# First block: modulation rows summed over partitions by accumulating DMAs on GpSimd, through a scratch row, in place of TensorE

## The reference

```python
cond = jax.nn.silu(c)                       # (1, 1024)
for l in range(2):
    mod = cond @ ada_w[l] + ada_b[l]        # 1024 x 9216
    sh1, sc1, g1, sh2, sc2, g2, sh3, sc3, g3 = jnp.split(mod, 9, axis=-1)
    hn = rms_norm(h, norm_g[l, 0]) * (1 + sc1) + sh1
    h = h + 0.5 * g1 * swiglu(hn, ffn1_w_in[l], ffn1_w_out[l])
    hn = rms_norm(h, norm_g[l, 1]) * (1 + sc2) + sh2
    h = h + g2 * (mixers(hn @ w_in[l]) @ w_out[l])
    hn = rms_norm(h, norm_g[l, 2]) * (1 + sc3) + sh3
    h = h + 0.5 * g3 * swiglu(hn, ffn2_w_in[l], ffn2_w_out[l])
```

## Time and profile before

| | us |
|---|---|
| median of 3 runs | 2239.07 |
| lowest and highest run | 2237.37, 2240.9 |
| profiled execution, device time | 2241.53 |
| its span, first to last instruction | 2239.8 |
| TensorE busy | 2187.2 |
| VectorE busy | 1589.0 |
| ScalarE busy | 1097.1 |
| GpSimd busy | 52.5 |

### The profile page before, as it was taken

One profiled execution on the slowest core, in us unless ns is written; L12 is line 12 of the kernel. 1 busy time (PEld: TensorE's weight loads), 2 busy tenths in 40 slices (PEclk: granted clock), 3 DMA queues, 4 the chain that ended last, 5 costly groups with the idle time before them and its releaser, 6 DMA issues.

```text
span 2239.8 us, 31962 instructions
## 1 busy us (share of the span) xinstructions
PE 2187.2 (98%) x11867; PEld 1843.9 (82%) x11867; DVE 1589.0 (71%) x1904; ACT 1097.1 (49%) x1288; POOL 52.5 (2%) x94
## 2 busy tenths in 40 slices
PE   7999999999999999999999999999999999999998
PEld 6887887887787897888788799978878879998887
DVE  5887898876777699665655778675575567867555
ACT  4344665444444466444544566554454446465443
POOL 1000010000000010000000000000000000000000
PEclk9999999999999999999999999999999999999999
DMA  8986576995687566665555464455556556435553
GB/s 283 345 315 219 162 225 209 327 315 173 242 291 244 155 212 197 229 224 192 185 190 192 154 167 132 151 188 187 187 173 203 187 169 169 133 132 170 191 191 104
DMA packets 325042, 454.56 MB, mean 203 GB/s; under 512 B 32722, under 2 KB 270040, under 8 KB 324952
## 3 DMA queue, kind: packets, MB, share of 16 engines
q1 hardware_dynamic: 320952, 440.98, 59.9%
q0 software_dynamic: 3728, 11.31, 1.7%
q10 hardware_dynamic: 272, 1.05, 0.1%
HBM read 449.91 MB, written 1.05 MB: 201 GB/s over the span
## 4 chain that ended last, share of the span: by engine, by line
PE 88%; DVE 6%; ACT 2%; issue 2%; DMA 1%; SPq 1%; DVEq 0%; ACTq 0%
PE ps L627 20%; PE ps L629 20%; PE ps L628 20%; PE ps L620 5%; PE ps L621 5%; PE ps L622 5%; PE ps L799 2%; DVE wlo L1993 1%; PE ps L781 1%; PE ps L784 1%; PE ps L782 1%; PE ps L718 1%; PE ps L1074 1%; ACT whi L1368 1%; DMA arena<-in_ada_w_dram 1%
## 5 line engine op out<-in xcount | busy, mean ns | idle before, releaser
L1993 DVE TENSOR_TENSOR wlo<-raw,whi 128x2048 fp32r<-128x2048 f32 x348 | 791.6, 2278 | 346.9 <-ACT whi L1368 345.4
L1368 ACT ACTIVATE whi<-raw 128x2048 fp32r<-128x2048 f32 x346 | 660.2, 1910 | 282.6 <-PE ps L629 241.5
L627 PE MATMUL ps<-whi,xl 128*128 128x512 f32 x1472 | 590.5, 401 | 0.0
L629 PE MATMUL ps<-whi,xh 128*128 128x512 f32 x1472 | 574.2, 390 | 0.0
L628 PE MATMUL ps<-wlo,xh 128*128 128x512 f32 x1472 | 574.0, 390 | 0.0
L627 PEld LDWEIGHTS ps<-whi,xl 128*128 128x128 f32 x1472 | 276.6, 188 | 61.6 <-issue 4.6
L629 PEld LDWEIGHTS ps<-whi,xh 128*128 128x128 f32 x1472 | 276.4, 188 | 60.0
L628 PEld LDWEIGHTS ps<-wlo,xh 128*128 128x128 f32 x1472 | 276.7, 188 | 57.5 <-issue 3.3
L627 PE MATMUL ps<-whi,hidl 128*128 128x512 f32 x640 | 252.1, 394 | 1.0 <-DVE hidl L2188 1.0
L620 PE MATMUL ps<-xl,whi 128*128 128x256 f32 x864 | 249.3, 288 | 1.6 <-DVE wlo L1993 1.6
L629 PE MATMUL ps<-whi,hidh 128*128 128x512 f32 x640 | 249.2, 389 | 0.0
(11 more groups left out here) (405 smaller groups left out, 2331.6 us busy)
## 6 DMA issues: line engine op xcount, KB each, us to landing
raw<-in_ffn_w_in_dram SPq DMA_DIRECT2D x176, 512.0 KB
arena<-in_ada_w_dram SPq DMA_DIRECT2D x144, 512.0 KB, 6.0
raw<-in_w_in_dram SPq DMA_DIRECT2D x54, 1024.0 KB
raw<-in_ffn_w_out_dram SPq DMA_DIRECT2D x44, 1024.0 KB
raw<-in_w_ffn_gate_dram SPq DMA_DIRECT2D x88, 512.0 KB
raw<-in_w_ffn_up_dram SPq DMA_DIRECT2D x88, 512.0 KB
raw<-in_w_ffn_down_dram SPq DMA_DIRECT2D x44, 1024.0 KB
raw<-in_w_out_dram SPq DMA_DIRECT2D x16, 1024.0 KB
```

Source lines behind the costliest of these rows:

```text
L627: pe.matmul(o, al, wh, start=start, stop=False, **kw)
L629: return pe.matmul(o, ah, wh, start=False, stop=stop, **kw)
L1368: act.activation(whi[:, k % 3, :], raw[:, k % 3, :], ACT.Copy).then_inc(hi_done, 1)
L1993: tt(a[0], a[1], a[2].bitcast(F32), ALU.subtract).then_inc(lo_done, 1)
```

## The change

In the feed-forwards n = 0, 2, 3 and 5 the sum over partitions is made by `fold_sums` on GpSimd. A DMA with an addition adds rows 64 to 127 of the accumulators onto rows 0 to 63, the next adds rows 32 to 63 onto 0 to 31, and so on, seven times, each step waiting for the one before. Row 0 is then stored to a scratch row in device memory, and each of its 1024-number pieces is loaded into all 128 partitions of its destination: shift, gate, and for the scale the buffer `adag`. `acc` is handled as two pieces of 1536 columns and `accg` as one of 1024, so that a step has three DMAs in n = 0 and 2, two in n = 3 and one in n = 5. VectorE waits for the rows after `lower_last(1)` and makes `gain` there, in one operation of 128 x 1024. The factor of 0.5 moves into `residual`. The matmuls, the waits for their banks, and the copies out of PSUM go in the feed-forwards; the mixers keep theirs.

```diff
-        SUMS = (0, 4, 10, 14, 20, 26, 30)
+        SUMS = (0, 4, 4, 8, 8, 8, 12)
+        LAID = {0: 64, 2: 128, 3: 176, 5: 192}
+        FOLDED = (0, 16 * 24, 16 * 48, 16 * 64)
...
-                if m not in (2, 5):
-                    pe.wait_ge(mod_read, SUMS[m] + q)
                 pe.matmul(ps[:, sumb(m, q), :], ones_row[:, :], acc[:, 512 * q:512 * q + 512], start=True,
...
-                    modulation(m, q)
...
-                    if q < 2:
-                        gate0(n, q)
...
-                    group(0, k, GROUPS - 3, (lambda q: modulation(m, q)) if m else None)
-                group(0, k + 3, GROUPS - 2, between1 if n == 0 else (lambda q: gate0(n, q) if q < 2 else None) if n in GATED else None, True)
+                    group(0, k, GROUPS - 3)
+                group(0, k + 3, GROUPS - 2, between1 if n == 0 else None, True)
...
-                if m:
-                    pe.wait_ge(mod_read, SUMS[m] + 6)
-                if n and n in GATED:
-                    pe.wait_ge(gate0_read, 2 * GATED.index(n) + 2)
...
-                st(tt(rtmp[:, f, :], o, gate[:, n % 2, 512 * f:512 * f + 512], ALU.mult))
+                st(stt(rtmp[:, f, :], o, 1.0 if n % 3 == 1 else 0.5, gate[:, n % 2, 512 * f:512 * f + 512], ALU.mult,
+                       ALU.mult))
...
                 lower_last(1)
-                if n in GATED:
-                    dve.wait_ge(gate0_read, 2 * GATED.index(n) + 2)
+                if n in LAID:
+                    dve.wait_ge(laid, LAID[n])
+                if m:
+                    dve.wait_ge(gain_loaded, 16 * m)
+                    st(stt(gain[:, :], adag, 1.0, gain[:, :], ALU.add, ALU.mult))
...
+            row_sums = nc.dram_tensor("row_sums", (4, 4 * D), F32, kind="Internal").ap()
+
+            def fold_sums(n):
+
+                e, m = list(LAID).index(n), n + 1 if n < 5 else 0
+                k, pieces = FOLDED[e], []
+                if m:
+                    until(adam_used, ADAM[m + 1] + 2)
+                    pieces += [(0, acc[:, 0:1536]), (1536, acc[:, 1536:3072])]
+                if n in GATED:
+                    until(adag_used, KC * (GATED.index(n) + 1) + 1)
+                    pieces += [(3 * D, accg)]
+                for half in (64, 32, 16, 8, 4, 2, 1):
+                    for _, t in pieces:
+                        pool.dma_start(t[0:half], t[half:2 * half], accum_op=ALU.add).then_inc(folded, 16)
+                        k += 16
+                    until(folded, k)
+                for at, t in pieces:
+                    pool.dma_start(row_sums[e:e + 1, at:at + t.shape[1]], t[0:1, :]).then_inc(folded, 16)
+                    k += 16
+                until(folded, k)
+                rows = [(3, gate[:, n % 2, :])] if n in GATED else []
+                if m:
+                    rows += [(0, shift), (1, adag), (2, gate[:, m % 2, :])]
+                for q, o in rows:
+                    pool.dma_start(o, row_sums[e, D * q:D * q + D].partition_broadcast(P)).then_inc(laid, 16)
+                until(laid, LAID[n])
...
                 if n == 5:
                     late_consts()
+                if n in LAID:
+                    fold_sums(n)
```

More of the change, by code:

```diff
@@ L220, in program @@
         mod_summed, mod_read = sem("mod_summed"), sem("mod_read")
-        gate0_summed, gate0_read = sem("gate0_summed"), sem("gate0_read")
+        folded, laid = sem("folded"), sem("laid")
         gain_loaded, gate_loaded = sem("gain_loaded"), sem("gate_loaded")
@@ L904, in between1 @@
                     if q == 3:
-                        pe.wait_ge(gate0_read, 2)
                         turn_setup(2)
@@ L1499, in summed @@
                 act.wait_ge(mod_summed, SUMS[m] + q + 1)
[L1500 to L1509, removed]
+                act.activation(shift[:, 512 * q:512 * q + 512], ps[:, sumb(m, q), :], ACT.Copy).then_inc(mod_read, 1)
             def ffn(L, n, j, k0):
@@ L1552, in ffn @@
                     setup_kept_out(0)
-                if m:
-                    summed(m, 0)
-                    summed(m, 1)
                 upper(g)
@@ L1562, in ffn @@
                     setup_exps()
[L1563 to L1567, removed]
+                    setup_kept_out(1)
                 hi(L, k + 7)
-                if n in GATED:
-                    gate0(n, 0)
-                    gate0(n, 1)
                 upper(g + 1)
@@ L2236, in ffn @@
                 product(g + 1, 0)
-                if m:
-                    summed(m, 2)
                 product(g + 1, 1)
-                if m:
-                    summed(m, 3)
                 lo(L, k + 6)
```

## The result

The changed kernel is slower by 3.5%, and its time lies outside the range given.

What follows compares the result with a forecast made beforehand. TensorE, busy 98% of the span, was taken to bound the kernel, with VectorE leading at boundaries. Folds against windows, savings and gain gave +5.5 us, the clock 3.5, total +9.0 on 2239.1: 2248 us, range 2221 to 2285.

Steps and rivals of the forecast that it cites:

- What goes: TensorE's sums in sub-blocks 0, 2, 3 and 5: 24 pairs of matmuls go at 0.86 us, 20.6 us.
- What comes on VectorE: Gain's multiply-add in sub-blocks 0, 2, 3: 1.28 us each, 3.84 us on the path; residual's two multiplications cost nothing.
- The window: From last addition to VectorE's last split: 42.0, 40.6, 42.25 and 36.2 us in sub-blocks 0, 2, 3 and 5.
- the formula: A sub-block's change is the larger of minus its saving and fold minus window, plus 1.28 us where gain is made.
- The length of a fold: On GpSimd, nine dependent steps: 44.8 us with three pieces, 38.6 with two, 28.9 with one.
- The prediction's own sign of being wrong: In GpSimd's chain, a small step under 3.2 us or over 5 would show the prediction wrong.
- A rule against the rows: Skill's 2.0 us plus bytes at 436 GB/s per DMA: folds of 36.2 and 29.5 us, sum -13.2 us, 2226 us.
- Additions that read twice: In the large halvings an addition also reads its destination; the middle was taken, 17.6 us together for three pieces.
- The clock: Behind late folds of sub-blocks 0 and 2 TensorE runs at a lower clock: 3.5 us, ends 0 and 7.
- What is queued behind: On GpSimd, clearing acc and its bias row stand behind the fold; 15.6 us are left for clearing, so covered.
- the rival of late weights: Fold and spreading traffic makes weights 3 us late in three sub-blocks: 9 us on top, about 2257 us; chance 5%.
- the one of dear accumulating DMAs: Accumulating DMAs much dearer than copies: folds 60.5, 53.5 and 42.3 us, +70 us, 2309 us; chance 20%.

Runs made afterwards that it cites:

- the run without waits: Changed kernel, but in sub-blocks 2 and 5 nobody waits for the fold, which works in a buffer nobody reads: 2277.39 us, ratio 1.0179.
- the small fold alone: Kernel before, with only the gate of sub-block 5 folded on GpSimd, one piece: 2247.6 us, ratio 1.0039.
- the appended chains of additions: Kernel before, with folds appended behind its output on idle DMA engines; time not compared, seven halvings of three pieces added took 42.5 us.

## Why the prediction was wrong, step by step

- **What goes**: right. TensorE's work of sub-block 0 ends 6.9 us earlier, counted from the last addition, as forecast (6.88), and the run without waits shows that it counts at the boundary.
- **What comes on VectorE**: right. Gain's operation takes 1.23 us (1.28 forecast), the residual's first operation with two multiplications 0.69 (0.683).
- **The window**: right. All four windows and the formula hold to 1 us, in the table above and for the small fold alone. One row under it was misread: 248.29 us is when the second half of x is turned, the first half was turned at 237.64. That a later start of VectorE's stretch delays TensorE by as much holds all the same.
- **The length of a fold**: this step failed, in the halvings. The store (3.15 us; 3.4 forecast) and the spreading (8.3; 8.3) were right. The halvings of three pieces were priced at 33.1 us and took 53.0. On idle DMA engines copies take 32.6 us, close to the 30.2 that my terms give for copies at no extra price; so the landings and the rule for size were fair for idle engines. What was missing is, first, the addition's own price. I had 2.9 us for it, as half of a second reading; it is 9.9 on idle engines, two thirds of it issuing. The 0.54 us for an issue came from plain DMAs and was carried over without an end to the range. Second, the traffic of its neighbours, for which I had nothing in the fold: another 10.5 us. The run with less weight traffic gives back 4.1 of these in sub-block 0 and 28.3 of 43.4 over the four folds; the rest isn't assigned. The landings of the earlier trace rows come from DMAs that nothing waits for one by one; here every step waits for the slowest of its three. A halving's DMA lands 4.4 us after its issue in the middle and 11.8 at most, in the appended chains of additions 3.2 and 7.2. The prediction's own sign of being wrong, a small step of over 5 us, came with 6.40 and 6.24.
- **A rule against the rows.** The Trainium skill, "DMA: Bandwidth & Descriptors", section "Anatomy of one DMA — SWDGE (gpsimd) path", came close for plain copies on idle engines: one piece, seven steps, 508 KB, with 0.3 us for each release, is 17.3 us by it (an estimate), and 18.6 were measured. For the halvings of sub-block 0 it is far off: 53.0 against the 26.3 (21.5 + 4.8) of the prediction's estimate; copies on idle engines took 32.6.
- **Additions that read twice.** "Collectives: The Full Stack" of the Trainium skill, section "The bandwidth ceiling: the fold count and why AG ≠ RS ≠ AR", has an adding transfer pay for two source reads. The runs show an addition dearer, but not in step with the bytes: on idle engines 1.70 us more than a copy in the first step of 1 MB, 1.09 in the last, which is one row of 16 KB in three pieces. Whether it reads twice can't be told from these numbers.
- **The clock**: of the size forecast or smaller. While TensorE stands, its granted clock is 0.50, the lower level of 1.2 GHz, and over the 10 us behind the first products it is 0.90, then 1.00:

```profile
252.40:262.00 9.60, 2.98 (x12) 2.17 (x12) 9.03 (x17) 3.84 (x6) 2.31 (x2) 0.50 0.01 3
262.00:272.00 10.00, 9.35 (x62) 7.73 (x60) 9.46 (x18) 6.50 (x12) 1.61 (x5) 0.90 0.11 13
272.00:282.00 10.00, 9.94 (x83) 9.94 (x84) 8.57 (x16) 5.05 (x8) 0.18 (x1) 1.00 0.65 208
```

  VectorE is busy for 9.03 of the first 9.60 us, so the slow TensorE follows it. The stretches behind the boundaries, where such a loss would stand, hold 3.0 us (0.95 + 2.0) with all else in them; 3.5 were forecast.
- **What is queued behind**: right. Clearing acc starts at 252.43 us, and the first addition that needs it at 271.73. None of ScalarE's waits for weights falls into the folds, so the rival of late weights did not come.
- **The rivals**: the one of dear accumulating DMAs came, with its time (2309 us) and its windows missed by 18.5, 19.9, 11.3 and 6.1 us, measured 23.1, 25.7, 15.7 and 4.8. Its cause was half of the truth: with additions turned into copies, the halvings were still almost as long; that its time came near is partly luck. It had 20%, and the range was cut below it; traffic had been weighed only for what the fold does to the weights, never for what the weights do to the fold.

## What to carry to other kernels

A chain of dependent DMAs is priced at the landings that it will meet, in the middle of its neighbours' traffic, and every step at the slowest of its DMAs; single landings on idle engines give the lower end only. A reduction over partitions by halving is seven such steps, 33 to 54 us in the changed kernel with one to three pieces of 4 to 6 KB a row in each and the weights' loads beside it, where TensorE needs 0.86 us for 512 columns (6.9 for the same 4096), or 0.47 with two bf16 parts. Before work is moved off the busiest engine, compare the new path's length with the time between its input and its first reader: here the formula of fold minus window held to a microsecond, and all depended on the length put into it.

## What was not expected of the hardware

- An adding DMA takes GpSimd longer to issue: three take 2.33 to 2.57 us (once 2.78, in the run with less weight traffic), three plain ones 1.43 to 1.57. One alone takes 0.76 to 0.88 against 0.49 to 0.56.
- Steps stay long after the traffic has gone. In this stretch of the changed kernel the DMA engines are busy for 0.07, and the step of two rows still takes 4.9 us, as on idle engines (4.91):

```profile
231.30:236.20 4.90, 0.00 (x0) 0.00 (x0) 0.00 (x0) 0.00 (x0) 2.41 (x3) 0.50 0.07 7
```

- The same fold of one piece took 41.0 us in one kernel and 44.6 in another. Its halvings took 33.3 and 37.4, with a DMA share of about two thirds in both: 0.67 and 0.66. What sets its length beyond that is open.
